# A step of a hybrid decoder layer: its last sum over expert rows by column halves, with the sample tile in second place

## What is computed

```python
def _moe(h, w_router, router_bias, w_gate, w_up, w_down, ws_gate, ws_up, ws_down):
    ...
    gates = jnp.einsum('tk,tke->te', wsel, jax.nn.one_hot(eidx, N_EXPERTS, dtype=wsel.dtype))

    def expert(acc, xs):
        wg, wu, wd, ge = xs
        y = (jax.nn.silu(x @ wg) * (x @ wu)) @ wd
        return acc + ge[:, None] * y.astype(jnp.float32), None

    routed, _ = lax.scan(expert, jnp.zeros((n_tok, shp[-1]), jnp.float32), (w_gate, w_up, w_down, gates.T))
    shared = (jax.nn.silu(x @ ws_gate) * (x @ ws_up)) @ ws_down
    return (routed + shared.astype(jnp.float32)).reshape(shp).astype(h.dtype)

def _layer(x, c, p, conv_buf, ssm0, fox_past):
    ...
    ffn = _moe(h2, w_router, router_bias, w_gate, w_up, w_down, ws_gate, ws_up, ws_down)
    x = _layernorm(DEEPNORM_ALPHA * x + gt2 * ffn, ln2_g, ln2_b)
    return x, (k_b.astype(x.dtype), v_b.astype(x.dtype), logf.astype(x.dtype), ssm_new, conv_new)
```

## Time and profile before

| | |
|---|---|
| runs | 1518.13, 1521.20, 1524.03 us; median 1521.2 us |
| span of the profiled execution, first to last instruction | 1515.0 us; its own time isn't recorded apart, the median of the runs lies 6.2 us above the span |
| TensorE busy over the span | 91% (1382.7 us) |
| VectorE, ScalarE, GpSimd busy | 37%, 19%, 21% |
| moved by DMA | 358.50 MB, mean 237 GB/s |
| the tail, from the first load's issue to the end | 1447.0 to 1515.0 us |

### The profile page before, as it was taken

One profiled execution on the slowest core, in us unless ns is written; L12 is line 12 of the kernel. 1 busy time (PEld: TensorE's weight loads), 2 busy tenths in 40 slices (PEclk: granted clock), 3 DMA queues, 4 the chain that ended last, 5 costly groups with the idle time before them and its releaser, 6 DMA issues. The chain is left out here.

```text
span 1515.0 us, 21977 instructions
## 1 busy us (share of the span) xinstructions
PE 1382.7 (91%) x8510; PEld 790.0 (52%) x8510; DVE 562.3 (37%) x1291; ACT 294.7 (19%) x677; POOL 314.4 (21%) x334
## 2 busy tenths in 40 slices
PE   5999999999979999899988799998999999999966
PEld 3876777764657777675444334443344343434322
DVE  2001465452724464455894334211121111111138
ACT  1002343443323321120121001111111111111021
POOL 6000000000079993000044111211111121111100
PEclk9999999999989999999999899999999999999988
DMA  9411310123464444674011989999999999999485
GB/s 338 172 56 39 111 58 0 70 71 112 137 183 141 137 139 115 240 258 166 35 43 49 399 348 411 401 416 415 421 395 403 409 421 400 406 402 421 188 314 226
DMA packets 106882, 358.50 MB, mean 237 GB/s; under 512 B 28915, under 2 KB 31091, under 8 KB 80659
## 3 DMA queue, kind: packets, MB, share of 16 engines
q1 hardware_dynamic: 81366, 301.98, 51.3%
q0 software_dynamic: 15968, 40.61, 7.3%
q10 hardware_dynamic: 9446, 14.51, 2.8%
HBM read 331.49 MB, written 38.15 MB: 244 GB/s over the span
## 5 line engine op out<-in xcount | busy, mean ns | idle before, releaser
L2132 PE MATMUL bank<-arena 128*32 128x512 f32 (+2 forms) x1536 | 338.1, 621 | 20.0 <-DMA arena<-in_w_up 19.2
L2132 PEld LDWEIGHTS bank<-arena 128*32 128x32 f32 (+2 forms) x1536 | 120.9, 139 | 204.8 <-issue 203.4
L2140 PE MATMUL bank<-arena 128*32 128x512 f32 (+2 forms) x768 | 168.6, 598 | 0.7 <-DVE arena L2886 0.7
L2119 POOL DMA_INDIRECT expert_rows<-arena x46 | 46.4, 1008 | 486.8 <-PE bank L2125 420.2
L2880 DVE TENSOR_TENSOR arena<-arena,bank 128x256 f32<-128x256 f32 x46 | 19.4, 421 | 324.1 <-ACT arena L2537 324.1
L1210 PE MATMUL bank<-arena 128*128 128x272 f32 x512 | 129.1, 405 | 0.7 <-ACT arena L1247 0.3
L438 PE MATMUL bank<-arena 128*128 128x272 f32 x480 | 113.9, 400 | 3.6 <-PEq L132 1.9
L2140 PEld LDWEIGHTS bank<-arena 128*32 128x32 f32 (+2 forms) x768 | 55.0, 134 | 110.3 <-issue 109.4
L1210 PEld LDWEIGHTS bank<-arena 128*128 128x128 f32 x512 | 96.0, 193 | 27.1 <-issue 6.1
L438 PEld LDWEIGHTS bank<-arena 128*128 128x128 f32 x480 | 93.0, 194 | 24.0 <-issue 2.8
L668 PE MATMUL bank<-arena 128*128 128x272 f32 x384 | 100.1, 405 | 0.0
(11 more groups left out here) (482 smaller groups left out, 1790.3 us busy)
## 6 DMA issues: line engine op xcount, KB each, us to landing
arena<-in_w_gate SPq DMA_DIRECT2D x64, 1024.0 KB
arena<-in_w_up SPq DMA_DIRECT2D x64, 1024.0 KB
arena<-in_w_down SPq DMA_DIRECT2D x64, 1024.0 KB, 15.2
arena<-in_w_ada SPq DMA_DIRECT2D x12, 2048.0 KB, 9.0
arena<-in_w_in SPq DMA_DIRECT2D x11, 2048.0 KB, 8.8
arena<-expert_rows SPq DMA_DIRECT2D x8, 2048.0 KB, 25.5
gate_logits<-arena ACTq DMA_DIRECT2D x16, 272.0 KB, 3.3
arena<-gate_logits SPq DMA_DIRECT2D x8, 544.0 KB, 5.0
```

What stands on the lines that cost most here:

```text
L2119: return nc.gpsimd.indirect_dma_start(out=y_d, out_offset=bass.IndirectOffsetOnAxis(ap=rows, axis=0), in_=of, in_offset=None, bounds_check ...
L2132: mm = nc.tensor.matmul(out[rows].rearrange("p (a n) -> p a n", a=2), x[:, k, rows], gate_up_slot(n)[:, :, k, :], start=k == 0, stop=k == ...
L2140: mm = nc.tensor.matmul(out[rows, :], h[:, k, rows], down_slot(n)[:, k, 512 * half:512 * half + 512], start=k == 0, stop=k == 1)
```

## The change

The order becomes first prompt tile, sample tile, other prompt tiles. `diagonals_before` holds how many diagonals must be made before each tile's sum, since the tiles no longer have a fixed step. On TensorE the loop over halves is now the outer one: all six products of the first 512 columns, then `sum_mm`, then the six of the second, then `sum_mm` again; a bank is waited for by half. VectorE takes each half on its own through the sum, the gate, the residual and the statistics; the closing two instructions are also made by halves, and each half tells `y_done`. SyncE stores each half of a tile on its own, 256 KB for a prompt tile. The sample tile's diagonals and banks are those of the second set.

```diff
--- before.py
+++ after.py
@@ -2078,7 +2078,8 @@
     acc = [at(T2, D), at(T2 + D, D)]
     diag = [at(d0 + 512 + P * i, P) for i in range(2 * NPE)]
     st2 = [at(d0 + 512 + 2 * P * NPE + 16 * i, 16) for i in range(2)]
-    TAIL = [PT, 0, 1, 2, 3]
+    TAIL = [0, PT, 1, 2, 3]
+    diagonals_before = [NPE, NPE + 8, 2 * NPE + 8, 3 * NPE + 8, 4 * NPE + 8]
     rows_s = at(T2 + 2 * D, 2, D)
     assert T2 + 4 * D <= WS0 + 3 * D
     assert DN_SLOT[4] + 2048 <= T2 and T2 + 2 * D <= WS0 + 3 * D and max(GU_SLOT) + SLOT <= X0
@@ -2197,9 +2198,11 @@
                 for h in range(2):
                     y_ld[t][h].inc(sp.dma_start(rows8[t][h][0:n], src[:, 4 * h:4 * h + 4, :]), 16)
             for i, t in enumerate(TAIL):
-                sp.wait_ge(y_done.sem, i + 1)
                 out = A["y_prompt"][0, P * t:P * t + P, :] if t < PT else A["y_sample"].rearrange("b t d -> (b t) d")
-                stored.inc(sp.dma_start(out, x_tm[0:TOKS[t], t, :]), 16)
+                for half in range(2):
+                    cols = slice(512 * half, 512 * half + 512)
+                    sp.wait_ge(y_done.sem, 2 * i + half + 1)
+                    stored.inc(sp.dma_start(out[:, cols], x_tm[0:TOKS[t], t, cols]), 16)
             sp.wait_ge(stored.sem, stored.n)
 
         @block.tensor
@@ -2436,24 +2439,23 @@
 
             for i, t in enumerate(TAIL):
                 n = TOKS[t]
-                pe.wait_ge(diag_done.sem, 8 + NPE * i)
-                if t == PT:
-                    pe.wait_ge(y_ld[t][0].sem, 64)
-                    for c in range(2):
-                        for half in range(2):
-                            mm = nc.tensor.matmul(bank[half][0:n, :], diag[c][:, 0:n], rows_s[:, c, 512 * half:512 * half + 512],
-                                                  start=c == 0, stop=c == 1)
+                pe.wait_ge(diag_done.sem, diagonals_before[i])
+                for half in range(2):
+                    cols = slice(512 * half, 512 * half + 512)
+                    out = bank[2 * (i % 2) + half][0:n, :]
+                    if i >= 2:
+                        pe.wait_ge(sum_rd.sem, 2 * (i - 2) + half + 1)
+                    if t == PT:
+                        pe.wait_ge(y_ld[t][0].sem, 64)
+                        for c in range(2):
+                            mm = nc.tensor.matmul(out, diag[NPE * (i % 2) + c][:, 0:n], rows_s[:, c, cols], start=c == 0, stop=c == 1)
+                    else:
+                        for k in range(NPE):
+                            if half == 0 and k % 4 == 0:
+                                pe.wait_ge(y_ld[t][k // 4].sem, 16)
+                            mm = nc.tensor.matmul(out, diag[NPE * (i % 2) + k][0:n, 0:n], rows8[t][k // 4][0:n, k % 4, cols],
+                                                  start=k == 0, stop=k == NPE - 1)
                     sum_mm.inc(mm)
-                    continue
-                if i >= 2:
-                    pe.wait_ge(sum_rd.sem, i - 1)
-                for k in range(NPE):
-                    if k % 4 == 0:
-                        pe.wait_ge(y_ld[t][k // 4].sem, 16)
-                    for half in range(2):
-                        mm = nc.tensor.matmul(bank[2 * (i % 2) + half][0:n, :], diag[NPE * (i % 2) + k][0:n, 0:n],
-                                              rows8[t][k // 4][0:n, k % 4, 512 * half:512 * half + 512], start=k == 0, stop=k == NPE - 1)
-                sum_mm.inc(mm)
 
         @block.scalar
         def _(act):
@@ -2570,12 +2572,12 @@
 
             def diagonals(i):
                 if i >= 2:
-                    act.wait_ge(sum_mm.sem, i - 1)
+                    act.wait_ge(sum_mm.sem, 2 * (i - 1))
                 if TAIL[i] == PT:
                     for c in range(2):
                         for q in range(4):
                             rows = slice(QUAD * q, QUAD * q + QUAD)
-                            diag_done.inc(nc.scalar.mul(diag[c][rows, 0:QUAD], ident[rows, rows], gates[rows, PT, 2 * q + c:2 * q + c + 1]))
+                            diag_done.inc(nc.scalar.mul(diag[NPE * (i % 2) + c][rows, 0:QUAD], ident[rows, rows], gates[rows, PT, 2 * q + c:2 * q + c + 1]))
                     return
                 for k in range(NPE):
                     diag_done.inc(nc.scalar.mul(diag[NPE * (i % 2) + k], ident, gates[:, TAIL[i], k:k + 1]))
@@ -2937,29 +2939,27 @@
                 n = TOKS[t]
                 a, st = acc[i % 2][0:n], st2[i % 2][0:n]
                 gate = lambda k: gates[0:n, t, k:k + 1]
-                dve.wait_ge(sum_mm.sem, i + 1)
-                if t < PT:
-                    dve.wait_ge(y_ld[t][1].sem, 16)
                 for half in range(2):
                     cols = slice(512 * half, 512 * half + 512)
+                    h = a[:, cols]
+                    dve.wait_ge(sum_mm.sem, 2 * i + half + 1)
                     if t == PT:
-                        ins = TT(a[:, cols], bank[2 * (i % 2) + half][0:n, :], gt2b[0:n, 1, cols], ALU.mult)
-                        done(sum_rd, ins) if half else step(ins)
-                        continue
-                    ins = STT(a[:, cols], rows8[t][1][0:n, 3, cols], gate(7), bank[2 * (i % 2) + half][0:n, :], ALU.mult, ALU.add)
-                    done(sum_rd, ins) if half else step(ins)
-                if t < PT:
-                    step(STT(a, rows8[t][1][0:n, 2, :], gate(6), a, ALU.mult, ALU.add))
-                    step(TT(a, a, gt2b[0:n, 0, :], ALU.mult))
-                step(TT(a, a, x_tm[0:n, t, :], ALU.add))
-                for j in range(2):
-                    step(nc.vector.bn_stats(st[:, 6 * j:6 * j + 6], a[:, 512 * j:512 * j + 512]))
+                        done(sum_rd, TT(h, bank[2 * (i % 2) + half][0:n, :], gt2b[0:n, 1, cols], ALU.mult))
+                    else:
+                        dve.wait_ge(y_ld[t][1].sem, 16)
+                        done(sum_rd, STT(h, rows8[t][1][0:n, 3, cols], gate(7), bank[2 * (i % 2) + half][0:n, :], ALU.mult, ALU.add))
+                        step(STT(h, rows8[t][1][0:n, 2, cols], gate(6), h, ALU.mult, ALU.add))
+                        step(TT(h, h, gt2b[0:n, 0, cols], ALU.mult))
+                    step(TT(h, h, x_tm[0:n, t, cols], ALU.add))
+                    step(nc.vector.bn_stats(st[:, 6 * half:6 * half + 6], h))
                 step(nc.vector.bn_aggr(st[:, 12:14], st[:, 0:12]))
                 done(var2, TS(st[:, 13:14], st[:, 13:14], LN_EPS, None, ALU.add))
                 dve.wait_ge(root2.sem, i + 1)
                 step(nc.vector.reciprocal(st[:, 13:14], st[:, 13:14]))
-                step(STT(a, a, st[:, 12:13], lng2[0:n], ALU.subtract, ALU.mult))
-                done(y_done, STT(x_tm[0:n, t, :], a, st[:, 13:14], lnb2[0:n], ALU.mult, ALU.add))
+                for half in range(2):
+                    cols = slice(512 * half, 512 * half + 512)
+                    step(STT(a[:, cols], a[:, cols], st[:, 12:13], lng2[0:n, cols], ALU.subtract, ALU.mult))
+                    done(y_done, STT(x_tm[0:n, t, cols], a[:, cols], st[:, 13:14], lnb2[0:n, cols], ALU.mult, ALU.add))
 
 
 IN = ["x_prompt", "x_sample", "c_prompt", "c_sample", "cache_k", "cache_v", "cache_logf", "state_ssm", "state_conv",
```

## The result

The changed kernel takes 1529.47 us (median of 18 runs, 1523.77 to 1532.33), the kernel before 1524.05 beside it (18 runs, 1518.13 to 1531.22). The ratio is 1.0039, with a 95% interval of 1.0027 to 1.0051: 5.9 us slower, between 4.1 and 7.8. The median difference is within half a per cent, and its sign is clear of noise. The forecast was 5.6 us more, 1526.8 us. It was built on the 1521.2 us of the three runs known then; with 18 runs the kernel before stands at 1524.05. This difference in the base, 2.85 us, and not one in the change, is why 1529.47 lies 2.7 us above the forecast, and above its narrower range of 1523.9 to 1528.5.

The account below looks back on a forecast made before the run. VectorE was taken to bound the tail, TensorE a close second. The terms -7.85 + 1.46 + 4.35 + 8.26 - 0.64 = +5.58 us gave 1526.8 us, 0.37% slower, at 0.62, with its own range of 1523.9 to 1528.5.

Parts of the forecast that it names:

- earlier start of VectorE's prompt tiles: Start of the tail: the first prompt tile's loads take the place of the sample's, so VectorE starts 7.85 us earlier.
- wait for the second half: First prompt tile: VectorE finishes the first half and waits 1.46 us for TensorE's sum of the second.
- halves in four prompt tiles: VectorE's prompt tiles: five instructions become two each, 1.09 us more a tile, 4.35 us for four.
- sample tile on the path: VectorE between two prompt tiles: the sample's work, no longer beside TensorE's first sums, adds 8.26 us.
- last store: End of the tail: the last store carries 256 KB where it carried 512 KB, 0.64 us less.
- (c): Rival on VectorE: halves cost nothing, 4.35 and 0.65 us fall away, 1521.8 us, no change; chance 0.10.
- (a): Rival at the tail's start: first load lands late, 10.1 us after issue, 2.3 us on the start, 1529.1 us; chance 0.15.
- (b): Rival at the tail's start: a tile's two loads land together, first half starts 4.9 us later, 1531.7 us; chance 0.06.
- (d): Rival behind the sample: TensorE's clock falls while it stands 3.1 us, next tile summed at 1.2 GHz, 1534.4 us; chance 0.04.
- The prediction's own objection: Against (d): if the clock came back as fast as in the first sum, five slow passes (2.1 us) would fit the slack.
- (e): Rival for the whole kernel: faster by over 0.5%, which would need something outside this stage; chance 0.03.

## Why the prediction was right

Its sum, term by term, in us, measured in the two profiled tails:

| term | predicted | measured | from |
|---|---|---|---|
| earlier start of VectorE's prompt tiles | -7.85 | -8.18 | 23.28 before, 15.10 after |
| wait for the second half | +1.46 | +1.43 | the row at 1475.25 |
| halves in four prompt tiles | +4.35 | +4.58 | 1526.10 - 1470.10 less the wait and the sample is 46.29; before 1512.01 - 1470.30 = 41.71 |
| sample tile on the path | +8.26 | +8.28 | 1483.08 to 1491.36 |
| last store | -0.64 | -0.59 | 2.99 behind VectorE's end before, 2.40 after |
| sum | +5.58 | +5.52 | 67.98 and 73.5 |

The mechanism came as forecast, term for term. That the sums agree to 0.06 us is luck: the start was 0.33 better and the halves 0.23 worse than forecast, and the two nearly cancel.

*The start.* The first load landed 7.25 us after its issue (7.8 taken from the branch weights), which is 0.55 better. The first eight passes took 5.73 us (1462.39 to the ninth at 1468.12) and not the 5.47 of the kernel before, which is 0.26 worse: the first pass was longer, 0.99 against 0.82, and the clock came back later. What I had not seen is how little room the second load has. The prediction had it land 4.9 us behind the first, at 12.7 us after the first issue, and treated it as being in time. In the changed kernel it landed 5.15 us behind the first, at 12.4, and was in time by 0.3 us. In the other three executions with this order it landed at 13.0 to 13.4 (12.7 to 13.0 us after its own issue), 5.7 to 6.0 behind the first. In the one without VectorE's work on the sample tile TensorE had to wait for it (0.52 us before the weight load where 0.24 is usual), and VectorE started at 15.20:

```profile
1471.08 0.34 PEld L2456 LDWEIGHTS bank<-arena 128*128 128x128 f32 x2 [0.52 <-DMA arena<-expert_rows]
```

So a warmer TensorE gave nothing, and by the same rows an earlier first load alone would have given next to nothing. By the Trainium skill, "DMA: Bandwidth & Descriptors", section "Anatomy of one DMA — SWDGE (gpsimd) path", the first load would have taken 6.8, an estimate from a formula that the page gives for transfers on GpSimd's path, while this load was issued by SyncE. The trace, at 7.25, lies between that and the row that I took.

*The halves.* The price per split was right to 0.02 us: 0.752 and 0.693 for the halves, against 0.746 and 0.692 from other lines of the kernel. Rival (c), free halves, is out by these rows, and by the kernel with the halves alone. The fixed part, an estimate of 0.157 us (151/0.96 ns) by the Trainium skill, "VectorE: DVE Perf Modes", section "The TRN2 errata — SBUF-src ops pay a fixed extra latency per instruction", fits the two-tensor form (2 x 0.693 - 1.226 = 0.16) and is too small for the form with a scalar (2 x 0.752 - 1.285 = 0.22).

*The sample.* In the profile before it looked free, since it stood in VectorE's wait. Moved, it cost its whole 8.28 us. The kernel with the order alone shows what else hung on it: there TensorE's wait for the diagonals joins in. In the whole change the halves end the first tile's statistics 3.1 us earlier (ScalarE's root comes 24.4 us after the first issue, against 27.5 with the order alone) and so keep that wait at 2.73 us instead of 5.84. The two parts are therefore not additive: the order alone costs 9.5, the halves alone 1.1, both together 5.5.

*The rivals.* (a) and (b), loads that land late or together, did not come: the first landed at 7.25 us, the second 5.15 behind it. (d), TensorE's clock falling behind the sample, did not come in the changed kernel, where it stood 2.73 us; it did where it stood 5.84, and then it cost 3.0 us of TensorE, not the 10.4 that I priced. The prediction's own objection (five slow passes, 2.1 us) was nearer: there were seven. (e) did not come.

No version tried beats the kernel before by anything that the times can tell.

## What to carry to other kernels

Before work is moved ahead of something, look at what its old place cost: the sample tile stood in a wait and was free, and in its new place, between two prompt tiles on the same in-order engine, it cost its whole 8.28 us. Splitting paid at the two ends of the chain, where it let the next engine start early or shortened the last store; in the middle, on an engine that is never idle, every split was its fixed time lost, 0.16 to 0.22 us on VectorE and 0.03 for the step to one more instruction. And an earlier start is worth only as much as what arrives next allows: with halves at the ends VectorE started 3.3 us earlier (19.99 against 23.28), and 2.22 of that went into a wait for TensorE one tile later.

## What the runs showed of the hardware

- TensorE's granted clock stayed at 2.4 GHz through a stand of 2.73 us and fell to 1.2 GHz in one of 5.84 us, late in it (1.00 from 1482 to 1486, 0.78 from 1486 to 1488, 0.50 behind); the next sums took 3.0 us longer.
- VectorE beside GpSimd: two instructions with two full operands in SBUF, the large on-chip memory, went from 1.28 to 3.25 us beside a GpSimd addition that had begun a microsecond earlier, and ended 1.1 us behind it; two others went to 2.02 and 1.89 beside a GpSimd product. Instructions that read one operand from PSUM kept their time (0.69 us each). By the Trainium skill, "SBUF — State Buffer", section "Who interferes with whom", a VectorE instruction with two inputs in SBUF contends with a GpSimd instruction that reads SBUF, since the second input comes through a read interface that both share. The trace agrees in part: others of the same form ran at 1.23 to 1.29 beside GpSimd in the same stretch, and why those were spared no run here shows.
- The same program ahead of the tail took 1447.0 us in one profiled execution and 1455.0 in another. A difference of a few microseconds has to be read from the stage that changed, from its own start, and not from the span.
